# Masking the log-factors of a stick-breaking attention on GpSimd instead of with a mask matmul ahead of the activations

## What is computed

```
z = einsum('bqhd,bkhd->bhqk', q, k) * scale
causal = s_idx[None, :] < t_idx[:, None]            # strictly before
log1m = where(causal, log_sigmoid(-z), 0.0)         # = -softplus(z)
after = cumsum(log1m, axis=3, reverse=True) - log1m # sum over j > s
logw  = where(causal, log_sigmoid(z) + after, -inf)
out   = einsum('bhqk,bkhd->bqhd', exp(logw), v)
```

## Time and profile before

| | |
|---|---|
| time, median of 3 runs | 3147.99 us (3146.27 to 3152.46) |
| time of the profiled execution | 3152.46 us |
| its span, first to last instruction | 3150.7 us |
| mean granted TensorE clock | 0.983 of full speed |
| PE busy | 3011.9 us, 96% |
| DVE busy | 2052.6 us, 65% |
| ACT busy | 1452.3 us, 46% |
| POOL busy | 160.8 us, 5% |

### The profile page before, as it was taken

One profiled execution on the slowest core, in us unless ns is written; L12 is line 12 of the kernel. 1 busy time (PEld: TensorE's weight loads), 2 busy tenths in 40 slices (PEclk: granted clock), 3 DMA queues, 4 the chain that ended last, 5 costly groups with the idle time before them and its releaser, 6 DMA issues.

```text
span 3150.7 us, 46760 instructions
## 1 busy us (share of the span) xinstructions
PE 3011.9 (96%) x16150; PEld 2553.6 (81%) x16150; DVE 2052.6 (65%) x3161; ACT 1452.3 (46%) x1964; POOL 160.8 (5%) x200
## 2 busy tenths in 40 slices
PE   6999899999899999999989999999999999999996
PEld 5888788888788888888878877888877888888885
DVE  5888666665665655555688885666666555556556
ACT  4555444544444444444455554555434444444442
POOL 5000011110000000000000000111100000000002
PEclk9999999999999999999999999999999999999998
DMA  8545567676465555555545545767664555555553
GB/s 269 156 136 150 134 179 194 176 197 213 155 220 187 186 186 186 186 186 186 172 134 156 148 137 147 199 180 201 199 219 147 187 186 186 186 186 186 186 187 120
DMA packets 672966, 562.12 MB, mean 178 GB/s; under 512 B 20760, under 2 KB 637568, under 8 KB 671872
## 3 DMA queue, kind: packets, MB, share of 16 engines
q1 hardware_dynamic: 668688, 548.48, 57.2%
q10 hardware_dynamic: 4208, 12.74, 1.1%
HBM read 552.78 MB, written 8.39 MB: 178 GB/s over the span
## 4 chain that ended last, share of the span: by engine, by line
PE 80%; DVE 9%; issue 4%; ACT 4%; POOL 1%; DMA 1%; ACTq 1%; DVEq 0%; POOLq 0%
PE banks L1400 20%; PE banks L1413 18%; PE banks L1401 10%; PE banks L1414 9%; PE banks L1422 5%; PE banks L1424 5%; PE banks L1423 5%; DVE lo L951 3%; ACT hi L627 2%; PE banks L1709 2%; PE banks L1710 1%; DVE hh L1365 1%; DVE hh L1361 1%; ACT pt L909 1%; DVE st L1098 1%
## 5 line engine op out<-in xcount | busy, mean ns | idle before, releaser
L951 DVE TENSOR_TENSOR lo<-raw,hi 128x1024 fp32r<-128x1024 f32 x1016 | 1206.7, 1230 | 307.9 <-ACT hi L627 278.6
L627 ACT ACTIVATE hi<-raw 128x1024 fp32r<-128x1024 f32 x880 | 886.1, 1051 | 354.5 <-PE banks L1424 236.4
L1413 PE MATMUL banks<-xs,hi 128*128 128x512 f32 x2816 | 1003.1, 400 | 16.5 <-DVE lo L951 7.7
L1400 PE MATMUL banks<-xs,hi 128*128 128x512 f32 x2544 | 903.3, 399 | 2.7 <-DVE lo L951 1.3
L1414 PE MATMUL banks<-xs,lo 128*128 128x256 f32 x2816 | 791.3, 281 | 0.0
L1401 PE MATMUL banks<-xs,lo 128*128 128x256 f32 x2544 | 711.0, 279 | 0.0
L1413 PEld LDWEIGHTS banks<-xs,hi 128*128 128x128 f32 x2816 | 531.7, 189 | 153.9 <-DVE lo L951 18.5
L1400 PEld LDWEIGHTS banks<-xs,hi 128*128 128x128 f32 x2544 | 478.6, 188 | 124.3 <-issue 9.7
L1414 PEld LDWEIGHTS banks<-xs,lo 128*128 128x128 f32 x2816 | 534.5, 190 | 0.8
L1401 PEld LDWEIGHTS banks<-xs,lo 128*128 128x128 f32 x2544 | 480.6, 189 | 0.2
L1422 PE MATMUL banks<-hi,hT 128*128 128x512 f32 x704 | 276.6, 393 | 8.2 <-DVE lo L951 8.2
(11 more groups left out here) (211 smaller groups left out, 2845.2 us busy)
## 6 DMA issues: line engine op xcount, KB each, us to landing
raw<-in_ffn_w_gate_up SPq DMA_DIRECT2D x176, 1024.0 KB, 5.1
raw<-in_w_in SPq DMA_DIRECT2D x160, 1024.0 KB, 6.4
raw<-in_ffn_w_down SPq DMA_DIRECT2D x88, 1024.0 KB, 5.3
raw<-in_w_o SPq DMA_DIRECT2D x32, 1024.0 KB, 5.4
raw<-in_mem_w_kv SPq DMA_DIRECT2D x16, 1024.0 KB, 5.8
raw<-in_sb_w_out SPq DMA_DIRECT2D x32, 512.0 KB, 4.2
raw<-in_ssm_w_out SPq DMA_DIRECT2D x32, 256.0 KB, 4.5
raw<-in_mem_w_out SPq DMA_DIRECT2D x32, 256.0 KB, 4.7
```

The lines of the kernel that those rows point to most:

```text
L627: act.activation(hi[:, hl_slot(ph, c, h), :], raw[:, slot, h * HALF:(h + 1) * HALF], ACT.Copy).then_inc(hi_ready, 1)
L951: dve.tensor_tensor(lo[:, s, :], raw[:, slot, h * HALF:(h + 1) * HALF], hi[:, s, :].bitcast(F32), ALU.subtract).then_inc(lo_ready, 1)
L1400: pe.matmul(dst[:, :], hi[:, s, w], x_t[:, k0 + k, :], start=first and k == 0, stop=False)
L1413: pe.matmul(bank[base + j], hi[:, s, w], xs[:, k, :], start=k == 0, stop=False)
```

## The change

The two mask matmuls leave `z(e)` and go to the end of `tri(e)`. The activations therefore see unmasked scores, and `sp_t` is no longer 0 at the masked places. A new constant, `causal` (1 where the key is strictly before the query, 0 elsewhere), is built on POOL, and POOL multiplies the two diagonal blocks of `sp_t` with it, in place, between DVE's step and `tri(e)`: one `tensor_tensor` on 128x256 elements for each head, in all 16. DVE now adds 1 to `sp_step` and POOL the other 1, and `tri(e)` waits for both as before.

```
@@ gpsimd, constants
+            pool.memset(causal[:], 1.0).then_inc(masks, 1)
...
-            pool.wait_ge(masks, 5)
+            pool.wait_ge(masks, 6)
...
+            pool.affine_select(out=causal[:], in_=causal[:], compare_op=ALU.is_gt, fill=0.0, base=0,
+                               pattern=[[1, P]], channel_multiplier=-1).then_inc(masks, 1)
@@ gpsimd, loop over the turns of the branch stage, after the product into prob
+                    for e in range(2):
+                        pool.wait_ge(sp_step, n * 4 + (2 * e + 3))
+                        v = sp_t[:].rearrange("p (a c) -> p a c", a=3)[:, 0:3:2, :]
+                        cm = causal[:].rearrange("p (a c) -> p a c", a=1).broadcast_to([P, 2, P])
+                        pool.tensor_tensor(v, v, cm, ALU.mult).then_inc(sp_step, 1)
@@ vector, softplus(e)
                         dve.scalar_tensor_tensor(out=sp_t[:], in0=Z[:, 0:384], scalar=0.0, in1=soft[:],
-                                                 op0=ALU.max, op1=ALU.add).then_inc(sp_step, 2)
+                                                 op0=ALU.max, op1=ALU.add).then_inc(sp_step, 1)
@@ vector and tensor, before their first use of the constants
-            pe.wait_ge(masks, 8)
+            pe.wait_ge(masks, 10)
@@ tensor, z(e)
                         pe.matmul(Z[:, T:384], k_f[:, P:T], q_f[:, P:T], start=False, stop=False,
-                                  skip_group_check=True)
-                        pe.matmul(Z[:, 0:P], ident_b[:], nbig[:], start=False, stop=False, skip_group_check=True)
-                        pe.matmul(Z[:, T:384], ident_b[:], nbig[:], start=False, stop=False,
                                   skip_group_check=True).then_inc(z_done, 1)
@@ tensor, tri(e)
-                        pe.matmul(Z[:, T:384], ntri[:], sp_t[:, T:384], start=False, stop=True,
+                        pe.matmul(Z[:, T:384], ntri[:], sp_t[:, T:384], start=False, stop=False,
+                                  skip_group_check=True)
+                        pe.matmul(Z[:, 0:P], ident_b[:], nbig[:], start=False, stop=False, skip_group_check=True)
+                        pe.matmul(Z[:, T:384], ident_b[:], nbig[:], start=False, stop=True,
                                   skip_group_check=True).then_inc(tri_done, 1)
```

More of the change, by code:

```diff
@@ L221, in trunk @@
         nones = sb("nones", [P, P])
+        causal = sb("causal", [P, P])
         nbig = sb("nbig", [P, P], BF16)
@@ L935, in _ @@
                 dve.sem_inc(s, v)
-            dve.wait_ge(masks, 8)
+            dve.wait_ge(masks, 10)
             dve.tensor_copy(ident_r[:], ident[:]).then_inc(consts, 1)
```

## The result

| | median us | runs | ratio to before, 95% interval |
|---|---|---|---|
| changed kernel, first measurement | 3177.76 | 4 | 1.0087 [1.0068, 1.0105] |
| before, beside it | 3150.22 | 4 | |
| changed kernel, second measurement | 3178.09 | 5 | 1.0078 [1.0064, 1.0092] |
| before, beside it | 3153.35 | 16 | |

The change makes the kernel 0.8 to 0.9% slower, 27.5 us in the first measurement and 24.7 in the second. The forecast was 17.9 us more and 3166 us, with a range from 3157 to 3177. The measured 3177.76 us lies just above that range: the direction and the mechanism hold, the size is too small.

A forecast was written before the change was run, and what follows sets the result against it. PE was taken as the bound, already waiting for sp_t at every tri. Later tri 11.8, BL scan 1.0, moved matmuls 0.3 and low clock 4.8 made 17.9 us on 3147.99, about 3166 us; range 3157 to 3177.

The forecast's parts named there:

- What bounds: PE is busy 96% of the span and waits for sp_t at all 16 tri(e), 24.4 us in total.
- rival A: Some later wait of PE behind tri shrinks by what tri's wait grows, giving 3149 us; chance 0.05.
- Part 1: Mask matmuls moved from z(e) to tri(e): chain 0.12 us earlier, PE's stream 0.11 longer, net 0; 0.3 us allowed.
- Part 2: POOL's multiplication before tri(e): 0.70 us plus hand-overs, each tri 0.84 us later, 14 x 0.84 = 11.8 us.
- rival B: DVE's second scan instruction gets in first and POOL waits 0.43 us more per head: 3172, or 3177 us; chance 0.25.
- Part 3: DVE's scan beside POOL loses 0.5 us per head, hidden in BR, on the path in BL: 1.0 us.
- Part 4: Longer waits at tri(1) in BR put 3 more stretches at PE's low clock, 3 x 1.6 = 4.8 us.
- Part 5: One more memset and select on POOL in set-up, at most 0.5 us, hidden behind POOL's idle time.
- The sum: Whole kernel: 11.8 + 1.0 + 0.3 + 4.8 = 17.9 us, applied to the median 3147.99, about 3166 us.
- Rival C: Fewer PE stretches fall to the low clock, so the kernel gets faster, about 3142 us; chance 0.02.

The follow-up runs named there:

- early_after: Changed kernel with DVE's softplus(e) put ahead of the chunk split that stood before it; ratio to before 0.9964.
- move_only: Changed kernel without the POOL multiplication, so only the mask matmuls move and sp_t stays unmasked; ratio to before 1.0002.
- after_again: The changed kernel timed once more, unchanged; ratio to before 1.0078.
- nudge_before: Kernel before with three transposes of the identity into an unread bank ahead of each gate loop; ratio to before 1.0018.
- mask_twice: Changed kernel with POOL's multiplication done twice in a row, with a wait between; ratio to before 1.0129.

## Why the prediction was right in kind and too small in size

- **What bounds.** Right. The account of the `BR` turn (2.75 us idle, all at `tri`) said that a delay there could not be given back, and it wasn't: rival A is out. `early_after` shows the reverse, the same instruction at 1.7 us for all 16 heads once it lies ahead of the wait.
- **Part 1, the move, net 0.** Right within 1.2 us, by `move_only`. The chain's start was moved as worked out: `soft` now starts 0.42 us after the start of the last score product (92.44 to 92.86) and started 0.53 us after it before (92.69 to 93.22): 0.11 us earlier, put at 0.12.
- **Part 2, POOL.** Mis-sized. The instruction was put at 0.70 us, and measured 0.88 behind DVE's running scan instruction and 0.74 where DVE stood idle as it started (`early_after`). Of the miss of 0.18, 0.04 is the instruction itself and 0.14 the time behind DVE, a third of what rival B charged. The hand-overs were put at 0.14 us net and came to 0.07 at the first head (0.08 + 0.05 - 0.06). The term 14 x 0.84 = 11.8 measured 13.8.
- **Part 3, DVE beside POOL.** Right: DVE loses 0.48 us (951 against 476 ns), put at 0.5, and in `BR` it is hidden. In `BL` it is on the path as forecast: `y_part` starts 4.0 us after the end of `sp_t` where it started 3.5 after it, 0.5 us for each of the two. The Trainium skill's rule (page "SBUF — State Buffer", section "Who interferes with whom"), that two such instructions shut each other out and the one issued first wins, agrees with the trace in kind. The trace has less than a whole recorded instruction: DVE's second ends at 100.82, 0.28 us after POOL (100.54), although it takes 0.48 us alone.
- **Part 4, the clock.** Right in kind. Of the six `tri(1)` in `BR` five ran slow where four were forecast, and four in `after_again`. Its 4.8 us came to 7.5 in the first execution, half of the 15 us more at the low level, and to some 3 in the second, so the size of this term is as much luck as forecast.
- **Part 5, set-up.** Nothing shows: the last score product of the first head starts at 92.44 us against 92.69 before.
- **The sum, and the step that failed.** The branch stages were to lose 17.9 us and lost 20.5 and 19.8; the terms add up there (from the first `tri` of each layer on 11.9 for the waits, 1.0 for `BL` and 7.2 for the busy part of the low clock, 20.1 for 20.0 measured). The step that failed is the silent one behind "I apply the sum to the median": that the stages without a changed instruction keep their time, a term put at nothing without a reason, and that the median of three runs stands for before. Those stages took 8.8 and 10.2 us more in the two profiled executions; at the medians the difference of 27.5 and 24.7 us leaves 7.0 and 4.9 for them. And the three runs shown, 3147.99, stood 2.2 us under the before timed beside the changed kernel, 3150.22, and 4 to 5 us under those of the later sets, 3152.08 to 3153.35. The 11.9 us between 3165.9 and 3177.76 are thus 2.6 of branch stages, 7.0 of other stages and, the rest, the baseline. From 3153 the same working would have given 3171, and a range moved with it would have held the result. (In the chances, B's worst with all of the clock's 8 adds up to 3180, not 3179.)
- **Rival C** had the right suspicion, that PE's rate in untouched stages moves the time, but by the clock and for the better; it was mostly the pace at a clock of 1.00, and it went the other way.
- **Rival B** priced POOL's wait for DVE at 0.43 us, taking DVE's second scan instruction to get in first. The second one was shut out in all 16; what kept POOL was the rest of the first.

## What to carry to other kernels

An instruction put at the end of a chain for which the busiest engine already waits costs its full time, the hand-overs, and some clock, however idle its own engine is; the same instruction cost 1.7 us in place of 20 where the chain has slack, so look first whether the chain can be started or reordered earlier. Before pricing such a change, see which wait comes next when the present one is gone: here 1.5 of 2.2 us came back at the next one. For effects below 1% compare the stages that were edited, not only the totals, and take the spread of the totals from more than three runs.

## What the runs showed of the hardware

- In the gate loops PE works through float32 pairs of 512 and 256 columns at one of two paces, 346.7 and 353.3 ns a pair, at the same granted clock of 1.00, and keeps one for a whole loop in which it never waits: 355.0 or 361.8 us, nothing between, in the 26 loops of 13 profiled executions. In the feed-forward stages there are two as well, 67.8 and 68.1 us a turn, and there they change from turn to turn. What chooses the pace was not found.
- A wait of PE of 2 to 4 us may or may not be followed by the 1.2 GHz level. It was in 1 of 6 `tri(1)` of `BR` at 2.2 us before (2 of 6 in `move_only` and in `nudge_before`), in 7 of 8 at 2.3 to 2.4 us (`tri(0)` of `mask_twice`), in 5 of 6 and 4 of 6 at 3.2 us (changed kernel, `after_again`), and in 6 of 6 at 4.0 to 4.1 us (`mask_twice`).
- POOL's two-input instruction takes 743 ns for 256 columns if DVE stands idle as it starts. Released 0.16 us into a DVE instruction with two SBUF inputs, 256 columns take 882 and 128 take 610, so a column costs about 2.1 ns. An estimate from the page "GPSIMD Engine Reference" of the Trainium skill (section "Elementwise — side-by-side cycle accounting"), 2.6 cycles at 1.2 GHz, is 2.2 ns. The trace agrees, and shows a fixed part of about 0.2 us beside it (743 - 256 x 2.1).
